# Neighbourhood attention: value key tiles moved by eight grid columns, two per query block; one exp and one eviction per block; negated scores; keys stored once, hi over lo

## The reference

```python
def row_block(r):
    ...
    s_loc = jnp.einsum('bqhd,bikhd->bhqik', q_r, k_b) + bias[None]
    s_loc = jnp.where(col_valid[:, None, :], s_loc, -jnp.inf)
    s_ctx = jnp.einsum('bqhd,bchd->bhqc', q_r, kc)
    p = jax.nn.softmax(jnp.concatenate([s_loc.reshape(b, NA_HEADS, GRID_W, n_loc), s_ctx], axis=-1), axis=-1)
    ...
    return jnp.einsum('bhqik,bikhd->bqhd', p_loc, v_b) + jnp.einsum('bhqc,bchd->bqhd', p_ctx, vc)
```

## Time and profile before

| | |
|---|---|
| median of 3 runs | 2043.54 us (2041.8 to 2045.07) |
| span of the profiled execution, first to last instruction | 2041.3 us |
| TensorE busy | 2002.5 us, 98% |
| VectorE busy | 1332.5 us, 65% |
| ScalarE busy | 735.7 us, 36% |
| layer 1's attention, first scores to last values | about 1318 to 1624 us |

### The profile page before, as it was taken

How to read it: one execution, slowest core, us unless ns; L and a number is a source line. 1 busy time by engine, 2 the same in 40 slices (tenths; PEclk the granted TensorE clock), 3 DMA queues, 4 the chain that set the end, 5 groups by cost and what they waited for, 6 DMA issues and landing times.

```text
span 2041.3 us, 29743 instructions
## 1 busy us (share of the span) xinstructions
PE 2002.5 (98%) x10776; PEld 1714.4 (84%) x10776; DVE 1332.5 (65%) x2240; ACT 735.7 (36%) x1271; POOL 96.0 (5%) x162
## 2 busy tenths in 40 slices
PE   8999999999999999999999999999999999999998
PEld 8888888888888888888888888788888778788886
DVE  7876635735645687766664567877887677557376
ACT  5423223323313343312331233555665543234133
POOL 0000000000000000000000000211111000000000
PEclk8999999999999999999999999999999999999999
DMA  7231311321231223233334324311111223223233
GB/s 296 75 101 62 114 63 53 103 70 59 82 102 52 62 68 97 93 124 114 92 103 124 103 93 152 123 48 42 57 42 43 89 77 103 93 93 103 86 99 103
DMA packets 51272, 186.60 MB, mean 91 GB/s; under 512 B 5680, under 2 KB 5680, under 8 KB 51184
## 3 DMA queue, kind: packets, MB, share of 16 engines
q1 hardware_dynamic: 37744, 136.73, 20.6%
q0 software_dynamic: 13440, 48.63, 7.7%
HBM read 181.15 MB, written 4.19 MB: 91 GB/s over the span
## 4 chain that ended last, share of the span: by engine, by line
PE 86%; DVE 7%; issue 3%; ACT 2%; DMA 1%; SPq 0%; DVEq 0%; ACTq 0%; POOLq 0%
PE acc L402 59%; PE acc L663 4%; PE o_ps L537 3%; PE o_ps L573 3%; PE o_ps L708 3%; PE acc L537 2%; PE acc L560 2%; PE o_ps L723 2%; PE acc L502 2%; PE acc L723 1%; DVE pt_lo L1778 1%; PE acc L758 1%; PE acc L696 1%; PE o_ps L688 1%; DMA ada_start<-in_ada_first_dram 1%
## 5 line engine op out<-in xcount | busy, mean ns | idle before, releaser
L871 ACT ACTIVATE w_hi<-raw 128x1024 fp32r<-128x1024 f32 x223 | 235.6, 1056 | 584.2 <-PE acc L402 467.2
L1292 DVE TENSOR_TENSOR w_lo<-raw,w_hi 128x1024 fp32r<-128x1024 f32 x223 | 272.8, 1223 | 256.4 <-ACT w_hi L871 254.5
L402 PE MATMUL acc<-h_hi,w_hi 128*128 128x512 f32 x1520 | 434.5, 349 | 3.7 <-issue 1.9
L402 PE MATMUL acc<-h_hi,w_lo 128*128 128x512 f32 x1520 | 434.8, 349 | 0.0
L402 PE MATMUL acc<-h_lo,w_hi 128*128 128x512 f32 x1520 | 434.7, 349 | 0.0
L402 PEld LDWEIGHTS acc<-h_hi,w_hi 128*128 128x128 f32 x1520 | 244.3, 188 | 44.0 <-ACT u L1072 2.5
L402 PEld LDWEIGHTS acc<-h_hi,w_lo 128*128 128x128 f32 x1520 | 244.4, 188 | 39.1
L402 PEld LDWEIGHTS acc<-h_lo,w_hi 128*128 128x128 f32 x1520 | 243.6, 188 | 38.4
L1461 DVE SCALAR_TENSOR_TENSOR x<-acc,mod,x 128x512 f32<-128x512 f32 (+3 forms) x137 | 82.0, 634 | 151.1 <-PE acc L402 120.9
L402 PE MATMUL acc<-act_hi,w_hi 128*128 128x512 f32 (+1 forms) x396 | 120.1, 357 | 2.0 <-DVE x L1461 2.0
L402 PE MATMUL acc<-act_hi,w_lo 128*128 128x512 f32 (+1 forms) x396 | 120.0, 357 | 0.0
(11 more groups left out here) (265 smaller groups left out, 3540.5 us busy)
## 6 DMA issues: line engine op xcount, KB each, us to landing
raw<-in_weights_dram SPq DMA_DIRECT2D x232, 512.0 KB, 3.5
ada_raw<-in_ada_dram POOLq DMA_DIRECT2D x80, 512.0 KB, 3.8
ada_start<-in_ada_first_dram SPq DMA_DIRECT2D x8, 1024.0 KB, 19.4
x<-in_x_in_dram SPq DMA_DIRECT2D x4, 768.0 KB, 7.1
park_dram<-x POOLq DMA_DIRECT2D x1, 2048.0 KB, 8.4
rel<-in_bias_dram POOLq DMA_DIRECT2D x16, 128.0 KB, 2.4
x<-park_dram POOLq DMA_DIRECT2D x2, 1024.0 KB, 6.8
out_dram<-x SPq DMA_DIRECT2D x8, 256.0 KB, 2.2
```

Of the source, the lines that this page charges most:

```text
L402: mm = nc.tensor.matmul(tile[:, c0:c0 + cn], wt[:, b * P:(b + 1) * P], mv[:, n, c0:c0 + cn], start=(n == 0 and m == 0), stop=(n == last an ...
L871: nc.scalar.activation(w_hi[i][:, :] if spare is None else spare[0], raw[r][:, :], ACT.Copy).then_inc(hi_split, 1)
L1292: nc.vector.tensor_tensor(lo, raw[r][:, :], hi.bitcast(F32), ALU.subtract).then_inc(lo_split, 1)
```

## The change

The four latent value tiles are moved by eight grid columns (64 keys), the last one wrapping around, so that each holds keys that only two query blocks see: tile 0 blocks 0 and 1, tile 1 blocks 1 and 2, tile 2 blocks 2 and 3, tile 3 blocks 0 and 3. `take_values` writes the values with the first 64 keys repeated behind the latent ones, and `turn_pair_values` reads them 64 columns on. Every block now has two key tiles and two context tiles: four transposes, and `probs_hi` and `probs_lo` are one instruction each. In `pair_values` each latent tile takes 256 columns; for tile 3 they are two runs of 128 with a step of 384. The probabilities of a block lie in one row of 512, so `exps` is one instruction with one sum, and L1766 goes. The scores are stored negated and their minimum is taken, so L1761 and a memset go. The keys are stored once, hi over lo (`nk`), and the queries twice (`nq_hi` on both halves, `nq_lo` on one half over zeros): the keys are emptied by one instruction per head on ACT and DVE in place of two, the queries' hi part by two per head in place of one. GpSimd zeroes one more buffer before the stage. The core of the diff:

```diff
 WIN = ((0, 24), (8, 32), (24, 32), (40, 24))
-TILES = ((0, 2), (0, 3), (1, 3), (2, 2))
+KEY_SLOTS = ((1, 0, 2, 3), (0, 1, 2, 3), (1, 0, 2, 3), (2, 3, 0, 1))
...
             x = sb("x", [P, KC, TOK], stack=part)
-        pt_hi = sb("pt_hi", [P, TT, QB * P], F32R)
-        pt_lo = sb("pt_lo", [P, TT, QB * P], F32R)
+        pt_hi = sb("pt_hi", [P, 4, QB * P], F32R)
+        pt_lo = sb("pt_lo", [P, 4, QB * P], F32R)
+        room = sb("room", [P, 4 * QB * P])
...
             rel = [sb(f"rel{i}", [P, 256], stack=stage) for i in range(2)]
-            nq = sb("nq", [P, 2, LAT], F32R, stage)
-            nk_hi = sb("nk_hi", [P, 2, TOK], F32R, stage)
-            nk_lo = sb("nk_lo", [P, 2, TOK], F32R, stage)
+            nq_hi = sb("nq_hi", [P, 2, LAT], F32R, stage)
+            nq_lo = sb("nq_lo", [P, 2, LAT], F32R, stage)
+            nk = sb("nk", [P, 2, TOK], F32R, stage)
...
             zeros = [nv_hi[:, :, :, :].bitcast(F32), nv_lo[:, :, :, :].bitcast(F32)] + [prob[a][:, :] for a in range(QB)]
-            zeros += [bias[i][:, :, :] for i in range(2)]
+            zeros += [bias[i][:, :, :] for i in range(2)] + [nq_lo[:, :, :].bitcast(F32)]
...
             def make_bias(hh):
 
-                for m, (lo, n) in enumerate(((64, 192), (0, 256), (0, 192))):
-                    nc.gpsimd.tensor_tensor(bias[hh][:, m, 0:n], rel[hh][:, lo:lo + n], masks[:, m, lo:lo + n], ALU.add)\
+                for m, (lo, n, at) in enumerate(((64, 192, 0), (0, 256, 0), (0, 192, CTX))):
+                    nc.gpsimd.tensor_tensor(bias[hh][:, m, at:at + n], rel[hh][:, lo:lo + n], masks[:, m, lo:lo + n], ALU.add)\
...
                 tile = o_ps[:, 1 + i % 2, :]
-                q = nq[:, hh, a * P:(a + 1) * P]
+                queries = [z[:, hh, a * P:(a + 1) * P] for z in (nq_hi, nq_lo)]
                 w0, wn = WIN[a][0] * ROWS, WIN[a][1] * ROWS
-                for c0, k0, n in ((0, w0, wn), (wn, LAT, CTX)):
-                    for m, nk in enumerate((nk_hi, nk_lo)):
+                for c0, k0, n in ((0, w0, wn), (wn, LAT, CTX)) if a < QB - 1 else ((0, LAT, CTX), (CTX, w0, wn)):
+                    for m, q in enumerate(queries):
...
                 tile = open_at(0)
-                for t in range(TILES[a][1] + 2):
-                    mm = nc.tensor.transpose(tile[:, t * P:(t + 1) * P], prob[a][:, t * P:(t + 1) * P], ident)
+                for t, to in enumerate(KEY_SLOTS[a]):
+                    mm = nc.tensor.transpose(tile[:, to * P:(to + 1) * P], prob[a][:, t * P:(t + 1) * P], ident)
...
                 pe.wait_ge(acc_taken[0], A.taken[0].now())
+                by_block = lambda z: z.rearrange("p (a q) -> p a q", q=P)
+                blocks = lambda z, t: z if t >= 4 else by_block(z)[:, 0:QB:QB - 1, :] if t == 3 else z[:, t * P:(t + 2) * P]
                 for n, t in enumerate((4, 5, 0, 1, 2, 3)):
-                    a0, a1 = (0, QB) if t >= 4 else (max(0, t - 1), min(QB, t + 2))
+                    slot = t - 2 if t >= 4 else t % 2
                     for m, (vt, pt) in enumerate(((nv_hi, pt_hi), (nv_hi, pt_lo), (nv_lo, pt_hi))):
-                        mm = nc.tensor.matmul(o_ps[:, 0, a0 * P:a1 * P], vt[:, t, hh, :], pt[:, t, a0 * P:a1 * P],
+                        mm = nc.tensor.matmul(blocks(o_ps[:, 0, :], t), vt[:, t, hh, :], blocks(pt[:, slot, :], t),
...
                 for t in range(TT):
-                    mm = nc.tensor.transpose(tile[:, t * P:(t + 1) * P], S[2][:, t * P:(t + 1) * P], ident)
+                    c0 = 64 + t * P
+                    mm = nc.tensor.transpose(tile[:, t * P:(t + 1) * P], S[2][:, c0:c0 + P], ident)
...
             def exps(i):
                 hh, a = divmod(i, QB)
-                wn = WIN[a][1] * ROWS
-                c0 = WIN[a][0] * ROWS - TILES[a][0] * P
-                c1 = TILES[a][1] * P
-                act.wait_ge(max_done, maxima.up())
-                nc.scalar.activation(prob[a][:, c0:c0 + wn], S[i % 2][:, 0:wn], ACT.Exp, bias=top[:, i % 2, 1:2],
-                                     accum_out=top[:, i % 2, 2:3])
-                nc.scalar.activation(prob[a][:, c1:c1 + CTX], S[i % 2][:, wn:wn + CTX], ACT.Exp, bias=top[:, i % 2, 1:2],
-                                     accum_out=top[:, i % 2, 3:4]).then_inc(exp_done, 1)
+                n = WIN[a][1] * ROWS + CTX
+                c0 = 64 if a == 0 else 0
+                act.wait_ge(s_taken, maxima.up() + 1)
+                nc.scalar.activation(prob[a][:, c0:c0 + n], S[i % 2][:, 0:n], ACT.Exp, bias=top[:, i % 2, 0:1], scale=-1.0,
+                                     accum_out=top[:, i % 2, 1:2]).then_inc(exp_done, 1)
             def probs_hi(i):
...
                     act.wait_ge(npv_done, values_done.now() + 1)
-                t0, tn = TILES[a]
-                nc.scalar.activation(pt_hi[:, t0:t0 + tn, a * P:(a + 1) * P],
-                                     tile[:, 0:tn * P].rearrange("p (t q) -> p t q", q=P), ACT.Copy)
-                nc.scalar.activation(pt_hi[:, 4:6, a * P:(a + 1) * P],
-                                     tile[:, tn * P:(tn + 2) * P].rearrange("p (t q) -> p t q", q=P), ACT.Copy)\
-                  .then_inc(pt_hi_done, 1)
+                nc.scalar.activation(pt_hi[:, :, a * P:(a + 1) * P], tile[:, 0:4 * P].rearrange("p (t q) -> p t q", q=P),
+                                     ACT.Copy).then_inc(pt_hi_done, 1)
             def take_values():
                 _, tile = wait_at(1)
-                nc.scalar.activation(S[2][:, 0:TOK], tile[:, 0:TOK], ACT.Copy).then_inc(acc_taken[1], 1)
+                nc.scalar.activation(S[2][:, 0:LAT], tile[:, 0:LAT], ACT.Copy)
+                nc.scalar.activation(S[2][:, LAT:LAT + 64], tile[:, 0:64], ACT.Copy)
+                nc.scalar.activation(S[2][:, LAT + 64:TOK + 64], tile[:, LAT:TOK], ACT.Copy).then_inc(acc_taken[1], 1)
...
             def take_keys(i, hh, full, splits=1):
...
                     act.wait_ge(acc_full, full)
-                for half in range(2):
-                    nc.scalar.activation(nk_hi[half * ND:(half + 1) * ND, hh, :], acc[i][hh * ND:(hh + 1) * ND, 0:TOK],
-                                         ACT.Copy).then_inc(n_hi_done, 1)
+                nc.scalar.activation(nk[0:ND, hh, :], acc[i][hh * ND:(hh + 1) * ND, 0:TOK], ACT.Copy).then_inc(n_hi_done, 1)
...
             def take_queries():
...
                 for hh in range(2):
-                    nc.scalar.activation(nq[0:ND, hh, :], o_ps[hh * ND:(hh + 1) * ND, 3, :], ACT.Copy, scale=ND ** -0.5)\
-                      .then_inc(n_hi_done, 1)
+                    for half in range(2):
+                        nc.scalar.activation(nq_hi[half * ND:(half + 1) * ND, hh, :], o_ps[hh * ND:(hh + 1) * ND, 3, :], ACT.Copy,
+                                             scale=ND ** -0.5).then_inc(n_hi_done, 1)
...
                 dve.wait_ge(s_full, score_tiles.up())
-                nc.vector.memset(top[:, i % 2, 5:6], 0.0)
-                nc.vector.tensor_tensor_reduce(S[i % 2][:, 0:n], o_ps[:, 1 + i % 2, 0:n], bias[hh][:, MASKS[a], 0:n], 1.0, -3e38,
-                                               ALU.add, ALU.max, top[:, i % 2, 0:1]).then_inc(s_taken, 1)
-                dve.wait_ge(s_taken, score_tiles.now() + 1)
-                nc.vector.tensor_scalar(top[:, i % 2, 1:2], top[:, i % 2, 0:1], -1.0, None, ALU.mult).then_inc(max_done, 1)
+                nc.vector.tensor_tensor_reduce(S[i % 2][:, 0:n], o_ps[:, 1 + i % 2, 0:n], bias[hh][:, MASKS[a], 0:n], -1.0, 3e38,
+                                               ALU.add, ALU.min, top[:, i % 2, 0:1]).then_inc(s_taken, 1)
             def scale_probs(i):
                 dve.wait_ge(exp_done, exps_made.up())
-                step(nc.vector.tensor_tensor(top[:, i % 2, 4:5], top[:, i % 2, 2:3], top[:, i % 2, 3:4], ALU.add))
-                step(nc.vector.reciprocal(top[:, i % 2, 4:5], top[:, i % 2, 4:5]))
-                nc.vector.tensor_scalar(prob[i % QB][:, :], prob[i % QB][:, :], top[:, i % 2, 4:5], None, ALU.mult)\
+                step(nc.vector.reciprocal(top[:, i % 2, 2:3], top[:, i % 2, 1:2]))
+                nc.vector.tensor_scalar(prob[i % QB][:, :], prob[i % QB][:, :], top[:, i % 2, 2:3], None, ALU.mult)\
...
             def probs_lo(i):
...
                 dve.wait_ge(pt_hi_done, pt_hi_made.up())
-                t0, normed = TILES[a]
-                for z0, zn, c0 in ((t0, normed, 0), (4, 2, normed * P)):
-                    hi, lo = (z[:, z0:z0 + zn, a * P:(a + 1) * P] for z in (pt_hi, pt_lo))
-                    ins = nc.vector.tensor_tensor(lo, tile[:, c0:c0 + zn * P].rearrange("p (t q) -> p t q", q=P),
-                                                  hi.bitcast(F32), ALU.subtract)
-                ins.then_inc(acc_taken[t], 1)
+                hi, lo = (z[:, :, a * P:(a + 1) * P] for z in (pt_hi, pt_lo))
+                nc.vector.tensor_tensor(lo, tile[:, 0:4 * P].rearrange("p (t q) -> p t q", q=P), hi.bitcast(F32), ALU.subtract)\
+                  .then_inc(acc_taken[t], 1)
```

(16 more changed lines are left out.)

8 lines of the change are left out of this document (4 added, 4 removed).

## The result

| | before | after |
|---|---|---|
| median of the runs | 2042.67 us (4 runs, 2040.63 to 2045.07) | 2025.79 us (4 runs, 2021.60 to 2026.71) |
| ratio, with its 95% interval | | 0.9909 [0.9898, 0.9921] |
| span of the profiled execution | 2041.3 us | 2023.9 us |

The changed kernel is 16.9 us faster, where 18.8 were forecast, and its median lies 1.1 us above the predicted 2024.7. The same kernel run a second time, among the experiments, gave 2024.56 and 0.9909 [0.9894, 0.9924]. Two executions, one of the kernel before and one in experiment 11, took 2.8 ms at a mean granted clock of 0.65; neither is in a ratio.

The account below looks back on a forecast made before the run. TensorE's own work was taken to set a pair's length, the rest being waits. Seven pairs' 16.9 us plus 2.9 for the last less 1.0 at the start gave 18.8, so 2024.7 us; range 2020.5 to 2034.

Parts of the forecast that it names:

- Work, 1.10 us a pair: TensorE in each pair: four transposes fewer save 0.44 us, narrower value matmuls 0.66; 8.8 us in eight pairs.
- tile 3 could cost two pieces: Rival, value matmuls: tile 3's stepped operand acts like two 128-column pieces, 5.8 us less gain, 2030.5 us; chance 0.08.
- Waits of 0.41 and 0.79 before blocks 2 and 6: TensorE's waits for `pt_lo` before these blocks' transposes: 0.41 us goes, and 0.79 of 0.84 goes, each pair.
- The reciprocal: DVE's reciprocal runs unheld beside GpSimd; the rival has it held, 0.43 us lost in seven pairs, 2027.7 us, chance 0.11.
- what GpSimd holds up is L1766 and L1768: DVE before block 2: GpSimd's bias additions hold the row-sum addition (for 0.43 us) and the scaling, not the reciprocal.
- Keys once and the wait of 0.20 before the scores: At a pair's end: the 0.20 us wait for the queries goes and none replaces it, with 0.05 us to spare.
- The new wait: TensorE before block 3: three value copies on ACT and an earlier block 2 bring a wait of about 0.12 us.
- idle places of half a microsecond between other blocks: Sign on TensorE's timeline: idle places of this size between other blocks would show the prediction wrong.
- The forecast of 2.4: Gain per pair with a follower: 0.44 + 0.66 + 0.41 + 0.79 + 0.20 - 0.12 + 0.04 = 2.4 us; seven give 16.9.
- The last pair: Last pair of the stage: 1.8 of 2.7 us without TensorE's work goes, and 1.1 of work: 2.9 us.
- the stage begins 1.0 us later: Stage start: four query copies on ACT move the first scores from 1317.64 to 1318.6, a cost of 1.0 us.
- the rival on the clock: Rival: TensorE's granted level falls from 2.4 to 1.2 GHz for part of the stage, doubling its work's time; slower, chance 0.04.

Follow-up runs that it names:

- experiment 11: Changed kernel with 11 identity products in the first pair's wait for the queries, and values emptied by ACT and DVE together: 2022.49 us, 0.9898.
- Experiment 3: Changed kernel with TensorE's old work given back (four more transposes a pair, 384 columns in two value tiles a head): 2032.3 us, 0.9950.
- experiment 4: Kernel before with only TensorE's work reduced (four transposes for each block, 256 columns in each latent tile): 2039.59 us, 0.9981.
- experiment 7: Kernel before with GpSimd's three bias additions per head cut to one column each from the second pair on: 2045.71 us.
- experiment 8: Changed kernel with a one-column addition of two SBUF operands, read by nobody, kept ahead of the reciprocal: 2024.12 us.
- experiment 9: Changed kernel with two one-column multiplications ahead of the reciprocal, pushing it past GpSimd's start: 2028.71 us.
- experiment 2: Changed kernel with the old storing of keys (high and low in two tiles) and queries (once): 2024.98 us, 0.9918.
- Experiment 5: Changed kernel with the values emptied by one ACT copy of 768 columns in place of three, the repetition left out: 2021.85 us.
- experiment 10: The changed kernel run and profiled again, with nothing altered: 2024.56 us.
- experiment 1: Changed kernel with 20 identity matmuls of 128 columns in TensorE's idle time ahead of the first pair's scores: 2023.86 us.
- experiment 6: Changed kernel with the last 256 columns of the values copied by DVE while ACT copies the rest: 2026.25 us.

## Why the prediction was right, and where it was not

**Work, 1.10 us a pair.** Right in size for tile and count (256 transposes, tile 3's rows as short as its neighbours'). Experiment 3 gives 0.92 for the part that it puts back. That tile 3 could cost two pieces is refuted: the rows with the stepped operand start 0.12 us apart like the others, and the group's mean is 281 ns.

**Waits of 0.41 and 0.79 before blocks 2 and 6.** Right, to 0.05: the way from block 1's transposes to block 2's is 0.48 us shorter where 0.52 was forecast, that from block 5's to block 6's 0.94 where 0.90 was. How they would end was right as well, with one detail off: the reciprocal does not start at the old place of L1766 but 0.19 us sooner, so that the scaling comes right behind GpSimd's start and is held for 0.36 us, where 0.23 were forecast (1444.82 to 1445.05). The slack was large enough for it. DVE's busy time in a pair fell by 6.1 us (30.32 to 24.25), where 5 were estimated. Which of the cuts in the chain (the negation, the sum, the second exp, the second `pt_lo` instruction) these two waits needed was not taken apart: experiments 3 and 4 separate the chain from the work, experiment 7 shows what GpSimd's hold was worth before, and experiment 8 that the sum alone no longer brings a wait back.

**The reciprocal.** The outcome was right, the argument for this kernel untested until experiment 9: after the change it simply ran ahead of GpSimd. The rival is refuted. The sentence "what GpSimd holds up is L1766 and L1768" is true of the kernel before, but L1766 was held only because it came 0.02 us behind GpSimd's start; experiment 8 brings it back a little earlier and it costs nothing.

**Keys once and the wait of 0.20 before the scores.** Right, and shown by experiment 2: with the doubled keys the wait is 0.39 in the new kernel; without, none. There is nothing to spare, though: in the fourth pair DVE ends the second `nq_lo` at 1468.18 and the scores start at 1468.29, the same 0.11 later as at the stage's start, where TensorE did wait for it.

**The new wait.** This step was wrong in place and size: "its slack before block 3 goes: a new wait of about 0.12 us there". I looked only at the chain through `pt_lo` and `acc[0]`. The wait is at `acc[1]`, between the values and the keys that follow them on TensorE, and it is 0.51 us a pair. Experiment 5 parts it: 0.17 for the three copies, 0.34 that one copy leaves; experiment 7 shows the latter uncovered in the kernel before as soon as block 2 comes earlier. Among the signs of a wrong prediction I had named idle places of half a microsecond between other blocks; this is one. A wait that is removed uncovers the next one, and I had made that check on one of the two accumulators only.

**Why the pair's length came out right all the same.** In the fourth pair 0.42 us too little were counted on the way from block 1 to block 3 (the new wait 0.38, block 2 0.04). Against them stand small terms, 0.50 us together, by which other steps came out shorter than forecast: those to blocks 0, 1 and 5 by 0.09, 0.08 and 0.05 where nothing was forecast, that to the first value matmuls by 0.09 in place of 0.04, to block 4 by 0.42 in place of 0.33, to block 6 by 0.94 in place of 0.90, to block 7 by 0.17 in place of 0.11, and 0.04 behind it. The forecast of 2.4 and the measured 2.50 (2.43 as a mean of the six) agree by errors that cancel. A part of the small terms is luck of another kind: the fourth pair has the longer form before and the shorter after. Form against form the gain is 2.3 us in the shorter (38.67 to 36.37) and 2.4 in the longer (38.87 to the 36.47 of experiment 10). I did not test the small ones.

**The last pair.** 3.5 in place of 2.9. Its time without TensorE's records fell from 34.45 - 31.76 = 2.69 to 30.91 - 29.87 = 1.04, so by 1.65 where I had counted 1.8; the term for the work is the one that was too small, 1.9 us by the records and not 1.1. The longest wait left is 0.8 us for the first `prob`, which the prediction had left standing (1.15 before). Why the records lost 1.9 was not tested; rows behind an idle place are longer than others (0.66 and 0.74 in the earlier trace rows, for 0.60 of four transposes), and there are fewer of these places.

**The first scores, "the stage begins 1.0 us later".** The microsecond is right (1.04). What it brought was not foreseen: the idle time ahead of the scores grew to 2.65 us, and the granted clock fell to 1.2 GHz for 3.2 us. I had argued against the rival on the clock that "the change takes idle time out"; that holds for the pairs, but at this one place it puts idle time in. The added copies cost 1.0 + 1.5 = 2.5 us and not 1.0. The rival counted on double the time at the lower level; measured are 0.64 us for 0.35, 1.8 times. That at this place the idle time is the cause is shown by experiment 1, which fills it alone, and by experiment 11 against experiment 6, which differ in the fill; that it is not chance, by all seven traces that have the idle time (experiment 10 is the same kernel again) and the six that have not.

**The rest of the difference.** The stage gained 18.6; the medians differ by 16.9, the profiled spans by 17.4; the profiled execution of the changed kernel took 2.8 us more than its span, where 2.2 had been carried over. Of what lies between, +2.5 us are ahead of the stage, and 2.0 of them are two more stretches at the lower clock, in code that the change doesn't touch (columns as in rows 2, in the trace after):

```profile
718.21:721.62 3.41, 3.41 (x15) 3.11 (x16) 0.49 (x2) 0.18 (x1) 0.00 (x0) 0.50 0.49 159
1284.82:1288.23 3.41, 3.41 (x16) 3.11 (x16) 1.07 (x6) 0.18 (x1) 0.00 (x0) 0.50 0.54 155
```

The trace before has neither. They cost 1.0 and 1.1 us, by the distances between the same rows in both traces; the remaining 0.5 had gathered by 714 us. Experiments 2, 6, 9 and 10 have both stretches, experiment 7, built on the kernel before, has one at 1290 us, and the others have none there, so this goes neither with the change nor against it. The last normalised tile stands between 1303.5 and 1312.8 in the twelve traces other than after's, before's kind and after's alike. Behind the stage, the stretch to the end takes 415.8 to 416.0 us in most kernels built on the changed one, but 416.7, 417.5 and 417.3 in experiments 2, 3 and 11. The last two have a stretch at a granted clock of 0.50 there (from 1646.49 and 1637.05), which costs 1.6 and 1.3 us and brings them to 415.9 and 416.0. What is left of the -1.3, 415.8 to 416.0 against the 416.6 to 417.1 of kernels built on the one before (and the 416.7 of experiment 2), is not settled; I made no test of it.

## What to carry over

When a wait is taken out of a loop, check the next limit on every buffer that the waiting engine shares with others, not only on the one that held it: here the second accumulator held 0.5 us a pair that had been invisible. Work that is taken off the busiest engine alone may count for half (experiment 4), and for much more once the chain beside it is shorter (experiment 3). And a microsecond more of waiting at a place where TensorE is already idle can cost more than itself (here 1.0 us brought 1.5 more); look for rows behind it at nearly twice their distance (here 0.64 for 0.35), and if they are there, cheap products that end just before the data arrives give the time back.

## What the hardware did that was not expected

**The clock after one idle stretch.** An idle time of 2.65 us, with TensorE busy before and behind, was followed by 3.4 us at a granted clock of 0.50, the level of 1.2 GHz, beginning 0.3 to 1.5 us after the restart, in all seven kernels that had it, and their first pairs were 1.5 to 1.7 us longer than the others. The other six, with two idle times of at most 1.1 and 0.5 us or with the idle time filled, had no such stretch there. What lies between was not tried.

**The same stretch with no idle time ahead.** The two stretches at 718 and 1285 us in the trace after came while TensorE was busy: in the 9 us ahead of each it was nowhere idle for more than 0.15 us. As they began it was running matmuls of 2 columns. The kernel before runs the same rows there at a granted clock of 1.00, and so do experiments 1, 3, 4, 5, 8 and 11. What decides there is open; a low stretch is not proof of idle time.

**How long GpSimd and DVE hold each other.** GpSimd's row of three additions is one of 192 columns, one of 256 and one of 192. Undisturbed they last 0.59, 0.73 and 0.59 us and start 0.56 and 0.69 apart. The scaling's end tells when it got going, as end less its own length (0.49 for 512 columns, 0.55 for 640), counted from the start of GpSimd's row. Issued 0.03 after that start it got going at 0.39 (after); issued at 0.22, at 0.39 (experiment 8); issued at 0.40, at once (experiment 9); the addition of before, issued at 0.02, at 0.46 (0.59 less its own 0.15). So the first addition held DVE for 0.4 to 0.46 of its 0.59 us. The second began at 0.56: the scaling of before, issued at 0.85, got going at 1.09, so it held DVE for 0.53 of its 0.73. It goes the other way too. The GpSimd addition that comes while DVE's scaling runs is longer, the second one after, the third one before (0.84 in place of 0.59):

```profile
L341 POOL TENSOR_TENSOR bias<-rel,masks 128x256 f32<-128x256 f32 x14 | 12.9, 920 | 0.0
```

The Trainium skill (SBUF — State Buffer, "Who interferes with whom") says of DVE's two-port modes that whoever issues first has the shared ports for the whole instruction and the other is blocked. The traces agree that each blocks the other. By GpSimd's rows the hold ends 0.13 to 0.2 us before the instruction does; spans of that engine are rough, and its instructions may end on the ports before they end in the profile.
